# Experts paired 16 apart, and the rows of the second last step kept in one half of the row store

## The reference, cut to what matters

```
x = x + g2 * moe(h2, ...)
p_grp = softmax(x32 @ wg + bg);  g_sel = argmax(p_grp)      # one of 4 groups
fine  = (x32 @ we + be) of that group;  top 2 of its 8 experts
act   = silu(hg) * hu * combine                              # each expert: 1024 -> 256 -> 1024
y     = sum over the two experts of act @ w_down
```

```
30 18 33 33 33 26 27 22 | 78 63 35 46 34 68 41 25 | 45 51 54 54 37 44 36 39 | 39 42 29 60 30 36 30 42
```

## Time and profile before

| what | us |
|---|---|
| median of 3 runs (lowest, highest) | 628.58 (627.99, 629.41) |
| the profiled execution's own time | 627.63 |
| its span | 625.6 |
| PE busy | 595.1 |
| DVE busy | 352.2 |
| POOL busy | 94.6 |
| mixture, first L1757 to last L1773 | 373.7 to 604.6 |

### The profile page before, as it was taken

How to read it: one execution, slowest core, us unless ns; L and a number is a source line. 1 busy time by engine, 2 the same in 40 slices (tenths; PEclk the granted TensorE clock), 3 DMA queues, 4 the chain that set the end, 5 groups by cost and what they waited for, 6 DMA issues and landing times.

```text
span 625.6 us, 9459 instructions
## 1 busy us (share of the span) xinstructions
PE 595.1 (95%) x3309; PEld 331.1 (53%) x3310; DVE 352.2 (56%) x788; ACT 177.4 (28%) x369; POOL 94.6 (15%) x131
## 2 busy tenths in 40 slices
PE   4999999999998999999999999999999999888987
PEld 1544555555565677645555545555555555445543
DVE  2745898765664987664666884334333433422446
ACT  4203887601144877731111101111111111111110
POOL 4000011121252000000000111122222212111200
PEclk9899999999999999999999999999999999988999
DMA  8999843330029628629213959999999999999978
GB/s 323 376 375 355 320 152 147 142 134 2 0 68 277 269 73 252 273 69 418 84 68 126 381 165 390 418 419 416 420 418 417 418 417 423 418 421 417 414 271 319
DMA packets 48273, 176.23 MB, mean 282 GB/s; under 512 B 10988, under 2 KB 18168, under 8 KB 34544
## 3 DMA queue, kind: packets, MB, share of 16 engines
q1 hardware_dynamic: 36992, 154.86, 63.5%
q0 software_dynamic: 6688, 15.58, 7.1%
q10 hardware_dynamic: 4560, 5.35, 2.4%
HBM read 163.31 MB, written 21.14 MB: 295 GB/s over the span
## 4 chain that ended last, share of the span: by engine, by line
PE 75%; DMA 13%; DVE 4%; SPq 4%; issue 1%; ACT 1%; ACTq 1%; POOL 1%; DVEq 0%; POOLq 0%
PE ps L1757 18%; PE ps L1574 11%; PE ps L1490 8%; PE ps L1773 8%; PE ps L1502 6%; DMA expert_w<-exp_w_up 5%; PE ps L1612 4%; PE ps L1639 4%; DMA gate_w<-lru_wx 3%; PE ps L1465 3%; PE ps L1621 3%; PE ps L1725 2%; SPq L358 2%; DMA recurrence<-w_mod 2%; PE ps L1411 1%; PE ps L1675 1%
## 5 line engine op out<-in xcount | busy, mean ns | idle before, releaser
L1757 PE MATMUL ps<-expert_w,hT_mixT 128*64 128x256 f32 x1120 | 136.4, 393 | 7.2 <-DMA expert_w<-exp_w_up 7.0
L1757 PEld LDWEIGHTS ps<-expert_w,hT_mixT 128*64 128x64 f32 x1120 | 84.0, 137 | 63.5 <-issue 19.5
L1490 PE MATMUL ps<-hT_mixT,w 128*128 128x128 f32 (+1 forms) x256 | 72.6, 437 | 1.2 <-DVE hT_mixT L918 1.2
L1574 PE MATMUL ps<-w,hT_mixT 128*128 128x512 f32 x160 | 71.9, 597 | 0.0
L1773 PE MATMUL ps<-expert_w,w 128*64 128x512 f32 x280 | 65.8, 598 | 0.0
L741 ACT ACTIVATE w<-ps 128x128 f32<-128x128 f32 x36 | 10.0, 278 | 188.6 <-PE ps L1757 188.6
L1490 PEld LDWEIGHTS ps<-hT_mixT,w 128*128 128x128 f32 x256 | 38.9, 191 | 35.8 <-issue 32.6
L1304 DVE SCALAR_TENSOR_TENSOR w<-w,ps 128x128 f32<-128x128 f32 x36 | 10.4, 288 | 82.3 <-ACT w L741 82.3
L1502 PE MATMUL ps<-w_qkv,hT_mixT 128*128 128x512 f32 (+1 forms) x160 | 53.2, 488 | 0.2 <-DVE v_tok L1006 0.2
L1322 DVE TENSOR_TENSOR w<-ps,w 128x1024 f32<-128x1024 f32 x17 | 20.8, 1225 | 56.5 <-PE ps L1773 56.5
L1574 PEld LDWEIGHTS ps<-w,hT_mixT 128*128 128x128 f32 x160 | 29.1, 191 | 29.9 <-issue 29.7
(11 more groups left out here) (289 smaller groups left out, 767.8 us busy)
## 6 DMA issues: line engine op xcount, KB each, us to landing
expert_w<-exp_w_down SPq DMA_DIRECT2D x31, 1024.0 KB
expert_w<-exp_w_gate SPq DMA_DIRECT2D x29, 1024.0 KB
expert_w<-exp_w_up SPq DMA_DIRECT2D x29, 1024.0 KB
w_mod_ring<-w_mod SPq DMA_DIRECT2D x14, 1024.0 KB, 6.5
y_rows<-zero_rows POOLq DMA_DIRECT2D x10, 512.0 KB, 9.2
expert_w<-y_rows SPq DMA_DIRECT2D x10, 512.0 KB, 6.9
recurrence<-w_mod SPq DMA_DIRECT2D x8, 512.0 KB, 10.0
w<-w_in SPq DMA_DIRECT2D x4, 1024.0 KB, 16.3
```

The source lines that it names most:

```text
L1490: ins = pe.matmul(ps[:, bank, 0:n], w1v[:, c, m * P:(m + 1) * P], HM[:, c, lo:lo + n], start=(c == 0), stop=(c == DC - 1))
L1574: ins = pe.matmul(ps[:, 2 * (t % 2) + half, :], HM[:, c, t * P:(t + 1) * P], w1v[:, c, half * 512:(half + 1) * 512], start=(c == 0), stop= ...
L1757: ins = pe.matmul(ps[r, 2 + k, 0:2 * P].rearrange("p (k f) -> p k f", k=2), xT[:, c, r], gate_up(i)[:, :, c, k:FF:FC], start=(c == 0), sto ...
```

## The change

- Pair q now has experts q and q+16 (`member`). With the same counts, the pairs with two steps are pair 8 (experts 8, 24) and pair 13 (13, 29). There are 18 steps again. The two experts of a pair are now of different groups, so no token has both choices in one pair.
- A token whose first choice is handled in the second last step (`late_step`) has its two rows exchanged: the first choice goes to the second half of the store, the second choice to the first half. So every row of the second last step lies in the second half. DVE computes this with three small operations ahead of `firsts`, which has twice the columns now; PE's sum over it has 10 matmuls for 5 (L1786).
- SP loads the first half to `yk` as soon as the scatter before the second last step has landed, and the second half to `y1` after the scatter of the second last step.
- The residual rows are added to the first half ahead of the last step's eviction: tiles 0, 1 and 2 on DVE (`base`), tiles 3 and 4 on POOL. After the eviction DVE adds `y1` for tiles 0, 2, 3, 4 (`with_late`), PE for tile 1 (`PE_SUMS = (1,)`).
- `chosen` is made ahead of the gating of the last step. The expert kept apart is 30, again the second of pair 14.

```diff
-PE_SUMS = (1, 2, 3)
+PE_SUMS = (1,)
+DVE_BASE = (0, 1, 2)
-KEPT = NE - 3
+KEPT = NE - 2
-        y0 = ring[:, 0, 0:NT * D].rearrange("p (t n) -> p t n", t=NT)
+        y1 = rf[:, NT * D:2 * NT * D].rearrange("p (t n) -> p t n", t=NT)
+        def member(q, i):
+
+            return q + PAIRS * i
...
                 for j in range(2 * s, 2 * s + both):
-                    w_gate_up(sp, q * 2 + (j - 2 * s), j)
+                    w_gate_up(sp, member(q, j - 2 * s), j)
...
+            end = sp.value_load(final[0:1, 0:1])
+            sp.wait_ge(S["y_out"], 16 * end)
+            sp.sem_inc(S["sp_turn"], 1)
+            for t in range(NT):
+                sp.dma_start(yk[:, t, :], a["y_rows"][t * P:(t + 1) * P, :]).then_inc(rows_in[t], 16)
             steps = sp.value_load(last[0:1, PAIRS - 1:PAIRS])
             sp.wait_ge(S["y_out"], 16 * steps)
             sp.sem_inc(S["sp_turn"], 1)
             for t in range(NT):
-                sp.dma_start(yk[:, t, :], a["y_rows"][TOK + t * P:TOK + (t + 1) * P, :]).then_inc(rows_in[t], 16)
-                sp.dma_start(y0[:, t, :], a["y_rows"][t * P:(t + 1) * P, :]).then_inc(y0_in[t], 16)
+                sp.dma_start(y1[:, t, :], a["y_rows"][TOK + t * P:TOK + (t + 1) * P, :]).then_inc(y1_in[t], 16)
...
             pool.wait_ge(S["xg_in"], 16 * (end + 2))
+            for t in range(len(DVE_BASE), NT):
+                pool.wait_ge(rows_in[t], 32)
+                row = yk[:, t, :].rearrange("p (c n) -> p c n", c=DC)
+                pool.tensor_tensor(row, row, x1_row(t), ALU.add).then_inc(S["base"], 1)
...
-            two = runs.rearrange("p (q e) -> p q e", e=2)
+            two = runs.rearrange("p (e q) -> p q e", e=2)
...
-            dve.tensor_scalar(firsts, hit[:, :, 0, :], -float(TOK), None, ALU.mult).then_inc(S["stepw"], 1)
+            step(dve.tensor_scalar(late_step, start[:, PAIRS:PAIRS + 1], -2.0, None, ALU.add))
+            step(dve.tensor_scalar(row_back[:, :, 1], stepno.rearrange("p (t k) -> p t k", k=TOP)[:, :, 0], late_step, -float(TOK),
+                                   ALU.is_equal, ALU.mult))
+            step(dve.tensor_scalar(row_back[:, :, 0], row_back[:, :, 1], -1.0, -float(TOK), ALU.mult, ALU.add))
+            dve.tensor_tensor(firsts.rearrange("p t k n -> p (t k) n"), hit.rearrange("p t k n -> p (t k) n"),
+                              row_back.rearrange("p t k -> p (t k)").unsqueeze(2).broadcast_to([P, TOP * NT, COLS]), ALU.mult)\
+               .then_inc(S["stepw"], 1)
...
             row_facts(end)
-            gated(end, 0)
-            gated(end, 1)
             dve.wait_ge(S["g2_in"], 16 * 3)
             dve.tensor_scalar(chosen, iota, now[:, 2:3], None, ALU.is_equal).then_inc(S["chosen"], 1)
+            gated(end, 0)
+            gated(end, 1)
+            for t in DVE_BASE:
+                base(t)
             last_y_evict(end)
-            with_second(0)
-            with_first(0)
-            with_second(1)
+            with_late(0)
             finish(0)
-            with_second(2)
+            with_late(2)
+            with_late(3)
             finish(1)
-            with_second(3)
-            with_second(4)
+            with_late(4)
             finish(2)
-            with_first(4)
             finish(3)
             finish_last()
```

More of the change, by code:

```diff
@@ L202, in build @@
         hit = W1[:, 232:232 + TOP * NT * COLS // 2].bitcast(F16).rearrange("p (t k n) -> p t k n", t=NT, k=TOP)
-        firsts = W1[:, 420:420 + (NT * COLS + 1) // 2].bitcast(BF16)[:, 0:NT * COLS].rearrange("p (t n) -> p t n", t=NT)
+        firsts = W1[:, 1812:1812 + TOP * NT * COLS // 2].bitcast(BF16).rearrange("p (t k n) -> p t k n", t=NT, k=TOP)
+        row_back = W1[:, 548:548 + TOP * NT].rearrange("p (t k) -> p t k", k=TOP)
+        late_step = W1[:, 560:561]
         rest = W1[:, 520:520 + TOP * NT]
@@ L241, in build @@
             "out_done v p act xg_in xt_mm gu_mm dn_mm xT_v xT_a th_ok act_ok aT_mm aT_ok y_v idxc_ok pidc_ok y_out "
-            "y_zero gu_half stepw w_mm now gsel chosen tail_mm fin sg_ok pool_turn sp_turn cache_out st_col st_t st_ev").split()}
+            "y_zero gu_half base stepw w_mm now gsel chosen tail_mm fin sg_ok pool_turn sp_turn cache_out st_col st_t st_ev").split()}
         rows_in = [sem(f"rows_in{i}") for i in range(NT)]
@@ L250, in build @@
         wd_in = [sem(f"wd_in{i}") for i in range(HELD)]
-        y0_in = [sem(f"y0_in{i}") for i in range(NT)]
+        y1_in = [sem(f"y1_in{i}") for i in range(NT)]
         used = dict.fromkeys(("v", "p", "act"), 0)
@@ L421, in _ @@
             for j in (0, 1):
-                w_gate_up(sp, j, j)
-                w_down(sp, j, j)
+                w_gate_up(sp, member(0, j), j)
+                w_down(sp, member(0, j), j)
             sp.wait_ge(S["bc_ok"], 1)
@@ L427, in _ @@
             for j in (2, 3):
-                w_gate_up(sp, j, j)
-                w_down(sp, j, j)
+                w_gate_up(sp, member(1, j - 2), j)
+                w_down(sp, member(1, j - 2), j)
             sp.wait_ge(S["x1"], 2 * LT)
@@ L452, in _ @@
             sp.wait_ge(S["xg_in"], 16)
[L453 to L454 removed]
+            sp.dma_start(ring[:, HOME[5], 0:EW], wg_v[member(2, 1)]).then_inc(wgu_in[2], 16)
+            w_down(sp, member(2, 1), 5)
             sp.wait_ge(S["ssq2"], 2 * NT)
@@ L479, in refill_in_halves @@
                             sp.dma_start(ring[:, HOME[j], lo + half * EW // 2:lo + (half + 1) * EW // 2],
-                                         src[q * 2 + (j - 2 * s), :, half * EW // 2:(half + 1) * EW // 2])\
+                                         src[member(q, j - 2 * s), :, half * EW // 2:(half + 1) * EW // 2])\
                               .then_inc(wgu_in[s] if half else halves_in, 16)
@@ L1198, in follow @@
                     step(dve.tensor_tensor(pre[:, (t + 1) % 2, :], pre[:, t % 2, :], pair[:, t, :], ALU.add))
-                both = ohk[:, t, :, :].rearrange("p k (q e) -> p k q e", e=2)
+                both = ohk[:, t, :, :].rearrange("p k (e q) -> p k q e", e=2)
                 step(dve.tensor_tensor(ohp[:, t, :, :], both[:, :, :, 0], both[:, :, :, 1], ALU.add))
@@ L1330, in _, with base, with_late @@
             end = every_step_but_last(dve, step_of)
-            def with_second(t):
+            def base(t):
                 dve.wait_ge(rows_in[t], 32)
                 dve.wait_ge(kept_in, 16 * (4 + SPILLED))
[L1335 to L1343, removed]
+                step(dve.tensor_tensor(yk[:, t, :], yk[:, t, :], x1b[:, t, :], ALU.add))
+            def with_late(t):
+                if t not in DVE_BASE:
+                    dve.wait_ge(S["base"], t - len(DVE_BASE) + 1)
+                dve.wait_ge(y1_in[t], 16)
+                step(dve.tensor_tensor(yk[:, t, :], yk[:, t, :], y1[:, t, :], ALU.add))
             def finish(t):
@@ L1785, in _ @@
             for t in range(NT):
-                ins = pe.matmul(ps[:, 6, 0:COLS], slot1[:, t, 0, :], firsts[:, t, :], start=(t == 0), stop=(t == NT - 1))
+                for k in range(TOP):
+                    ins = pe.matmul(ps[:, 6, 0:COLS], slot1[:, t, k, :], firsts[:, t, k, :],
+                                    start=(t == 0 and k == 0), stop=(t == NT - 1 and k == TOP - 1))
             ins.then_inc(S["idx_mm"], 1)
@@ L1815, in _ @@
                     if t in PE_SUMS:
-                        pe.matmul(ps[:, 2 * t % 8 + half, :], ident[:, :], y0[:, t, half * 512:(half + 1) * 512],
+                        pe.matmul(ps[:, 2 * t % 8 + half, :], ident[:, :], y1[:, t, half * 512:(half + 1) * 512],
                                   start=True, stop=False)
```

22 lines of the change are left out of this document (11 added, 11 removed).

## The result

| | median us | runs | lowest, highest |
|---|---|---|---|
| before | 628.58 | 5 | 627.99, 630.32 |
| changed | 635.04 | 5 | 635.01, 638.67 |
| changed, measured again beside the first experiments | 636.24 | 6 | 633.51, 636.98 |

The changed kernel is slower: the ratio is 1.0109 with a 95% interval of 1.0083 to 1.0134, and 1.0093 (1.0071 to 1.0115) the second time, where the kernel before had a median of 629.31. Forecast were 636.0 us and a range of 632 to 639.

What follows compares the result with a forecast made beforehand. It took the weight stream, 4.6 us per pair slower than PE, as what sets pair 13's arrival. 12.25 - 0.72 - 0.8 - 4.7 + 1.6 = +7.6 on 627.63 gave 635.2; as median 636.0 us, range 632.0 to 639.0.

Steps and rivals of the forecast that it cites:

- The second pass behind the last weights: At pair 13, now step 14: its second pass follows the last late arrival with nothing to hide it, +12.25 us.
- The start of the tail: Sum of the terms up to the tail: second pass, last wait gone, pair 13 earlier; +10.7 us.
- the slow matmuls behind its wait: L1757 at pair 13, slower after a wait: 8.83 us against 7.42, paid once as before.
- the work ahead of step 0: Added DVE and PE routing operations move step 0 by 0 to 0.3 us; PE's later waits swallow it: 0.
- Where PE waits: PE's waits for weights: near 464 and 481 us, again at pairs 11 to 13, near 20 us for 7.0.
- The tail: From the last eviction's start to the end: 16.1 us for 20.8, so -4.7.
- the faster rival: The stream hides pair 13's second pass, only the tail's saving stays: 625.5 us; chance 0.06 for faster by either way.
- The cover of the early loads: First half's rows land by 609 to 611 us, before the last eviction at 615.5; loads hidden, 0 to 2 us spare.
- The rival of the late landing: Step 16's scatter takes 9.8 us beside the first half's loads; PE and DVE wait 2 us: 638 us, chance 0.12.
- The collision: POOL's and DVE's residual additions before the last eviction exclude each other, delaying it 0 to 2.6 us, taken as +1.6.
- the rival without a collision: POOL is done before DVE starts, or the stream gains 1.4 us: +6.0 or less, 634 us, chance 0.22.
- 0.72: The wait before the last step goes, since pair 15's weights have a step more of time: -0.72 us.

Runs made afterwards that it cites:

- the control: The changed kernel with SP's loop of refills written out: 635.78 us, ratio 1.0091.
- the early order: The order of pairs in early_pairs: experts 8 and 13 fall in pairs 4 and 7, pairs still 16 apart.
- no_pool_adds: The changed kernel with POOL's two additions of residual rows for tiles 3 and 4 left out: 633.87 us.
- early_little_first: early_pairs with only 64 of 1024 columns of each tile of the store's first half loaded: 630.67 us, ratio 1.0033.
- early_pairs: The changed kernel, SP's refill loop written out, pairs reordered so experts 8 and 13 fall in pairs 4 and 7: 628.69 us, ratio 0.9992.
- early_late_load: early_pairs with the first half loaded behind the scatter of the second last step, ahead of the second half: 631.23 us, ratio 1.004.
- pairing_alone: The kernel before with the experts of a pair 16 apart and nothing else: 637.21 us, ratio 1.012.

## Why the prediction was right, and where not

- **The second pass behind the last weights, +12.25.** Right, and shown three ways: undone it gives back 7.5 us with the pairs still 16 apart; alone it costs 7.9 (637.21 for 629.31); with a light stream it costs nothing.
- **The start of the tail, +10.7.** Measured +11.55, and +11.1 with the pairing alone, but in part by luck. Two steps were wrong and nearly cancel. Pair 13 was forecast 0.8 us earlier, for a step fewer gathered and scattered, and came 1.6 later (1.1 with the pairing alone). And the slow matmuls behind its wait were to be paid "once, as before"; in the profile read here they weren't paid at all, 1.4 us less. In the first profile of the changed kernel they didn't cancel: pair 13 came 3.1 later, the matmuls behind its wait were slow (10.13 us), and the tail began 15.7 us later.
- **What pair 13's arrival goes with.** I had put the work ahead of step 0 at nothing, since PE's waits would swallow it. In eleven of twelve profiles with the full stream pair 13's first matmul stands 191.4 to 192.1 us behind step 0's, wherever step 0 stands (373.74 to 376.46); the pairing alone has 192.7. So what step 0 loses pair 13 loses too: 1.3 of the 1.6 us here, 0.3 of that the added routing work (2.34 us between the first L1744 and L1776 for 2.01 before). The rest was there before the first L1744, which stood at 372.73 here and at 371.70 in the control with the same routing. A gain from the step fewer shows nowhere: the kernels with it have 191.7 to 192.7, those without 191.4 to 191.8. Why it is missing stays open.
- **Where PE waits.** Forecast at pairs 7, 8 and 11 to 13 with near 20 us in all; found at pairs 6, 7, 8, 11, 12 and 13 with 14.9. A sum of waits doesn't show what PE loses in the matmuls behind them, 9.07 and 10.13 us for 7.42, 4.4 us more than unhindered; waits and slow matmuls together are 19.2 for 9.7 before.
- **The tail, -4.7.** The size is right (-4.9), but not whose it is: 1.7 us come from the late second pass, which lets the last scatter and the loads find an empty queue, and 3.2 from the change's own code. My statement of the faster rival, that only the tail's saving stays if the second pass is hidden, was therefore wrong by its whole amount: in the early order the saving isn't there (from PE's last transposes to the end 25.7 us for 25.9). It comes back, 4.0 us, only with the load and POOL's additions both taken away.
- **The cover of the early loads.** I gave the scatter of step 15 a landing time of 7.0 to 9.8 us. It took 7.3 (593.96 to 601.3), though by the counts it has 4 rows to write (expert 13's 68 less 64), where those two prices were of 66 and 89 rows: its own rows aren't what sets the time. The second last step's took 5.3 beside the first half's loads (4.0 in no_pool_adds), and 3.1 in an empty queue. The Trainium skill, DMA: Bandwidth & Descriptors, section Queues, rings and completion order, has each engine take turns between queues by the packet; by that rule my estimate is that a scatter beside one other queue at most doubles its time. The trace agrees for 5.3 against 3.1, but not for the 9.8 of the earlier trace rows. That one was issued while POOL's gather before it was still on its way (landed at 584.5), and no run takes the two apart. The rival of the late landing fell.
- **The collision, +1.6 of 0 to 2.6.** Right as a mechanism, and 1.7 us in the profile read here. Its price depends on when the rows land: nearly nothing in the first profile of the changed kernel, as the rival without a collision had it, and in early_little_first the eviction came 4.1 us late. So the range was too narrow above.
- **The sum.** 12.25 - 0.72 - 0.8 - 4.7 + 1.6 = 7.6 for 6.5 and 6.9 in the medians, and 8.4 between the profiles.

## What to carry to other kernels

Where weights stream through a ring more slowly than they are used, extra work is free only where it stands ahead of a late arrival; ask of every reordering which work lies behind the last wait for the stream. A transfer that is moved earlier gains only if the DMA engines are idle where it lands, so look at their share in that stretch first. And two engines that exclude each other on their operands should not be given the two halves of one job at the same moment.

## What the runs showed of the hardware that I had not expected

- DVE and POOL additions with both inputs in on-chip memory run one after the other: five that take 8.5 us by themselves took 7.8 together, and a DVE addition of 1.22 us beside one of POOL took 3.28. DVE's eviction, with one input from PE's accumulators, wasn't stretched: 1.29 us beside POOL's 2.35 in early_pairs. The Trainium skill, SBUF — State Buffer, section Who interferes with whom, says that DVE and GpSimd share one pair of ports as an exclusive lock, and that a DVE instruction with two SBUF inputs contends with a GpSimd one that reads SBUF. By that rule the five would take their sum, 8.5 us, and the trace agrees within 0.7.
- After an idle time of 4.5 us PE's granted clock fell to 0.50, the lower of its two levels (1.2 GHz), and stayed there for some 6 us; the 64 matmuls took 10.13 us. After idle times of 0.9 to 1.7 us they took 7.47. In between the length of the idle time doesn't decide it: 2.05 us in the control (unrolled) were followed by 9.07 us, 2.90 us in early_late_load by 7.47 with the clock at 1.00. The rows are of the first profile of the changed kernel:

```profile
568.49 10.13 PE L1776 MATMUL ps<-expert_w,hT_mixT 128*64 128x256 f32 x64 [4.50 <-DMA expert_w<-exp_w_up]
...
570.00:572.00 2.00, 2.00 (x14) 1.18 (x12) 0.00 (x0) 0.00 (x0) 0.00 (x0) 0.50 1.04 426
```

- An indirect scatter of 71 rows of 4 KiB landed in 3.1 us with the DMA engines otherwise idle (pairing_alone); one of 89 rows took 9.8 us with them full (the kernel before), and one of 4 rows 7.3 us while the stream of weights ran out (the changed kernel).
